# Five re-orderings around waits of TensorE in a two-stack transformer kernel

## What is computed

```
x = x + mamba2_mixer(rms_norm(x, a_norm), ...)   # ends in: groups of y normed, then y @ w_out
x = x + conv_ffn(rms_norm(x, ffn_norm[0]), ...)  # up_a, down
x = x + dilated_mixer(rms_norm(x, b_norm), ...)  # ends in: o @ w_o          (att_o)
x = x + conv_ffn(rms_norm(x, ffn_norm[1]), ...)
for l in range(2):
    h = h + mixer_sublayer(rms_norm(h), ...)
    h = h + memory_cross_attention(rms_norm(h), rms_norm(mem), ...)
    h = h + conv_ffn(rms_norm(h), ...)           # u = h @ w_up; silu(conv(gate)) * val; @ w_down   (up_b, down)
def _rms_norm(x, w, eps): return x * rsqrt(mean(x * x) + eps) * w
```

## Time and profile before

| what | us |
| --- | --- |
| median of 3 runs | 2086.16 |
| lowest and highest | 2086.12 and 2088.02 |
| the profiled execution | 2087.74 |
| its span, first to last instruction | 2085.9 |
| TensorE busy in it | 2067.2 |
| VectorE, ScalarE, GpSimd busy | 1666.1, 1058.4, 256.7 |

### The profile page before, as it was taken

One profiled execution on the slowest core, in us unless ns is written; L12 is line 12 of the kernel. 1 busy time (PEld: TensorE's weight loads), 2 busy tenths in 40 slices (PEclk: granted clock), 3 DMA queues, 4 the chain that ended last, 5 costly groups with the idle time before them and its releaser, 6 DMA issues.

```text
span 2085.9 us, 38628 instructions
## 1 busy us (share of the span) xinstructions
PE 2067.2 (99%) x16378; PEld 2016.3 (97%) x16378; DVE 1666.1 (80%) x2449; ACT 1058.4 (51%) x1282; POOL 256.7 (12%) x176
## 2 busy tenths in 40 slices
PE   9999999999999999999999999999999999999998
PEld 9999999999999999989999999999988999989998
DVE  8987888788769778898986768768698996748765
ACT  6886444457744435355545445434346445445432
POOL 0112055000004510001201001100000301000100
PEclk9999999999999999999999999999999999999999
DMA  7663544563325455443555434445554454534542
GB/s 263 197 205 144 184 182 172 179 216 142 122 102 193 160 188 214 172 181 142 199 186 175 169 142 176 176 165 212 182 182 142 182 185 181 182 131 174 196 144 104
DMA packets 58300, 361.95 MB, mean 174 GB/s; under 512 B 6736, under 2 KB 9360, under 8 KB 21136
## 3 DMA queue, kind: packets, MB, share of 16 engines
q1 hardware_dynamic: 58128, 359.48, 48.4%
HBM read 358.37 MB, written 1.08 MB: 172 GB/s over the span
## 4 chain that ended last, share of the span: by engine, by line
PE 94%; DVE 3%; ACT 1%; issue 1%; POOL 0%; DMA 0%; SPq 0%; DVEq 0%; ACTq 0%
PE acc L639 77%; PE acc L638 7%; PE acc L756 1%; PE acc L755 1%; PE acc L754 1%; DVE w_lo L1192 1%; PE acc L959 1%; ACT w_hi L2059 1%; PE pA L1008 1%; PE pC L802 0%; PE pB L1032 0%; PE pB L1119 0%; PE pD L1119 0%; PE pB L1094 0%; PE pA L1094 0%
## 5 line engine op out<-in xcount | busy, mean ns | idle before, releaser
L639 PE MATMUL acc<-in_hi,w_hi 128*128 128x256 f32 x4656 | 1306.7, 286 | 6.5 <-DVE in_hi L1280 3.8
L639 PE MATMUL acc<-in_hi,w_lo 128*128 128x256 f32 x4656 | 1295.8, 284 | 0.1
L639 PE MATMUL acc<-in_lo,w_hi 128*128 128x256 f32 x4656 | 1233.0, 284 | 0.0
L2059 ACT CAST w_hi<-raw 128x2048 fp32r<-128x2048 f32 (+1 forms) x341 | 615.4, 1805 | 634.8 <-PE acc L639 541.2
L1192 DVE TENSOR_TENSOR w_lo<-raw,w_hi 128x2048 fp32r<-128x2048 f32 (+1 forms) x341 | 739.5, 2169 | 229.3 <-ACT w_hi L2059 228.3
L639 PEld LDWEIGHTS acc<-in_hi,w_hi 128*128 128x128 f32 x4656 | 894.2, 192 | 10.0 <-DVE in_hi L1280 4.0
L639 PEld LDWEIGHTS acc<-in_hi,w_lo 128*128 128x128 f32 x4656 | 894.2, 192 | 0.6 <-DVE w_lo L1524 0.3
L639 PEld LDWEIGHTS acc<-in_lo,w_hi 128*128 128x128 f32 x4656 | 856.7, 192 | 1.2 <-issue 1.0
L2663 POOL TENSOR_TENSOR in_lo<-arena,in_hi 128x256 fp32r<-128x256 f32 (+1 forms) x112 | 139.0, 1241 | 1202.4 <-ACT in_hi L2521 509.9
L1839 DVE SCALAR_TENSOR_TENSOR arena<-arena,cols 128x256 f32<-128x256 f32 x480 | 200.3, 487 | 0.0
L2673 POOL TENSOR_TENSOR arena<-arena 128x256 f32<-128x256 f32 x44 | 84.7, 1925 | 393.0 <-ACT arena L2343 393.0
(11 more groups left out here) (293 smaller groups left out, 1629.3 us busy)
## 6 DMA issues: line engine op xcount, KB each, us to landing
raw<-in_wide SPq DMA_DIRECT2D x285, 1024.0 KB, 4.8
raw<-in_narrow SPq DMA_DIRECT2D x64, 704.0 KB, 4.0
arena<-cs_rows SPq DMA_DIRECT2D x16, 256.0 KB, 4.6
arena<-in_mem SPq DMA_DIRECT2D x3, 1024.0 KB, 4.8
x<-in_x SPq DMA_DIRECT2D x4, 256.0 KB, 6.2
raw<-in_wide SPq DMA_DIRECT2D x2, 512.0 KB, 5.8
tables<-in_tables SPq DMA_DIRECT2D x1, 1024.0 KB, 14.9
arena<-cs_rows SPq DMA_DIRECT2D x16, 64.0 KB, 5.6
```

The lines of the kernel that those rows point to most:

```text
L639: return mm(outs[m], w[:, k, at], moving[:, c, :], start=start, stop=stop)
L2059: copy(w_hi[s][:, 0:n], raw[g % RAW][:, 0:n]).then_inc(hi_ready, 1)
```

## The change

Five edits, all in the order of instructions or in the engine that does them. No matmul is added or taken away.

1. The low parts of the last two of the eight groups go from GpSimd to VectorE, behind its scaling of the groups and ahead of the split of the third `ssm_out` unit. A semaphore `group_low` signals them, and TensorE's late groups 6 and 7 wait on it.
2. `memory_stats` moves from behind unit 6 of the first `down` to behind unit 8, the root from unit 7 to 9, the reciprocal from 7 to 10.
3. In `att_o`, the split that stood between unit 2's early input and its sum of squares goes behind the last unit's early input, just ahead of the split that is there already.
4. In `ffn_b` ScalarE loads the silu table by a one-column activation (`silu_table`) right after the norm, ahead of the next unit's cast.
5. In `ffn_b` VectorE's `norm` leaves out `split(3)` (`leave=True`). It stands now behind the first unit's convolution, with that unit's multiplication (`second`) right behind it, and `split(4)` after both.

```diff
--- before.py
+++ after.py
@@ -363,6 +363,7 @@
         group_sq = sem("group_sq")
+        group_low = sem("group_low")
         rest_in = sem("rest_in")
@@ -455,7 +456,7 @@
             count["all"] += n
-            count[maker] += n
+            count[maker] += n - 2 if name == "groups" else n
@@ -889,7 +890,9 @@
                 early_groups = parts("groups", 0, 4, 2, gin_ready)
-                late_groups = parts("groups", 0, GROUPS_S, 2, gin_ready)[4:]
+                late_groups = parts("groups", 0, GROUPS_S - 2, 2, gin_ready)[4:]
+                late_groups += [(range(2 * g, 2 * g + 2), piece["groups"][0] + g + 1, group_low, g - GROUPS_S + 3)
+                                for g in (GROUPS_S - 2, GROUPS_S - 1)]
                 seg, unit, groups = units("ssm_out")
@@ -898,7 +901,7 @@
                 groups(1, early_groups)
-                E.passed(gin_ready, GROUPS_S)
+                E.passed(gin_ready, GROUPS_S - 2)
                 E.passed(y_ready, GROUPS_S)
@@ -916,7 +919,7 @@
             def memory_stats(u, j):
-                if j == 6:
+                if j == 8:
                     pe.wait_ge(sq_sum, 2)
@@ -1205,6 +1208,7 @@
                     banks = banks_of(seg.base + j)
+                    last_sum = name == "att_o" and u == seg.units - 1
                     fixed = isinstance(u, int)
@@ -1222,15 +1226,20 @@
                             scale_unit(seg, nth, 2)
+                        if early and u == 0:
+                            split(3, seg, 3)
+                            second(u, j, banks)
                         if u < 3:
...
                             split(9, seg, 9)
-                    if ahead and not late:
+                    if last_sum:
+                        split(u + 1, seg, j + 1)
+                    if ahead and not late and not (name == "att_o" and u == seg.units - 2):
                         split(u + 2, seg, j + 2)
-                    if second:
+                    if second and not (late and behind and early and u == 0):
                         second(u, j, banks)
@@ -1259,7 +1268,7 @@
                     tt(sq[:, 0, :], sq[:, 0, :], sq[:, 1, :], ALU.add).then_inc(sq_sum, 1)
-                if j == 7:
+                if j == 10:
                     reciprocal_std(rmem[:])
@@ -1387,7 +1396,7 @@
-            def norm(name, nth, chunk0=0):
+            def norm(name, nth, chunk0=0, leave=False):
@@ -1397,7 +1406,8 @@
                 scale_unit(seg, nth, 1)
-                split(3, seg, 3)
+                if not leave:
+                    split(3, seg, 3)
                 low_parts(xn, chunk0, NORM_PIECES, DC // NORM_PIECES, first=half)
@@ -1615,6 +1625,11 @@
                 group_scaled(1)
+                for g in (GROUPS_S - 2, GROUPS_S - 1):
+                    dve.wait_ge(inh_ready, piece["groups"][0] + g + 1)
+                    at = DC + 2 * g if g < 7 else 0
+                    tt(in_lo[:, at:at + 2, :], xbc[:, 2 * g:2 * g + 2, :], in_hi[:, at:at + 2, :], ALU.subtract
+                       ).then_inc(group_low, 1)
                 E.passed(inh_ready, GROUPS_S)
@@ -1667,7 +1682,7 @@
                 def run():
-                    norm(f"f_norm{l}", 5 + 3 * l)
+                    norm(f"f_norm{l}", 5 + 3 * l, leave=True)
                     hid0 = made["hid"][2 + l]
@@ -2352,7 +2367,7 @@
                     def beside(u, j, banks):
-                        if layer == 0 and j == 7:
+                        if layer == 0 and j == 9:
                             norm_root()
@@ -2361,9 +2376,15 @@
+            def silu_table():
+
+                E.settle()
+                E.mark(fn(act_scratch[:], wcol("eps_rms"), ACT.Silu))
+
             def ffn_b(l):
...
                     norm()
+                    silu_table()
                     base = take.base()
@@ -2700,9 +2721,9 @@
                     ssd_mask(g)
-                for g in range(GROUPS_S):
+                for g in range(GROUPS_S - 2):
                     pool.wait_ge(inh_ready, piece["groups"][0] + g + 1)
-                    d = slice(DC + 2 * g, DC + 2 * g + 2) if g < 7 else slice(0, 2)
+                    d = slice(DC + 2 * g, DC + 2 * g + 2)
                     tt(in_lo[:, d, :], xbc[:, 2 * g:2 * g + 2, :], in_hi[:, d, :], ALU.subtract).then_inc(gin_ready, 1)
...
```

## The result

| | median, us | lowest to highest | runs |
| --- | --- | --- | --- |
| before | 2086.92 | 2086.12 to 2088.02 | 6 |
| changed | 2080.28 | 2079.80 to 2080.63 | 6 |

The ratio is 0.9967, with a 95% interval of 0.9958 to 0.9977. The change takes 6.64 us off the median. The forecast was 2079.0 with a range of 2077.0 to 2082.2, so the time is 1.3 us above the forecast and inside its range. It lies at the very edge of the narrower range, 2077.8 to 2080.3, that the forecast was given for itself.

A forecast was written before the change was run, and what follows sets the result against it. TensorE, busy 2067.2 of 2085.9 us, bounds the kernel, so only its waits and the slow clock behind them count. 3.49 + 0.80 + 1.86 + 1.78 = 7.93 us gave 2079.8 or 2078.2; forecast the middle, 2079.0, range 2077.0 to 2082.2.

The forecast's parts named there:

- Edit 1, 3.49 us: Late groups: 1.90 us of wait and 1.59 us of half clock both go; bounds 0.3 and 3.49.
- the rule of exclusion: Late groups: two-input VectorE and GpSimd operations exclude each other for a whole instruction; VectorE's parts done at 197.1 and 197.75.
- Edit 2, 0.80 us: First `down`: TensorE's wait for the memory sum, matmul at 395.08 instead of 394.28, goes; bounds 0 and 0.80.
- Edit 3, 1.86 us of 5.52: `att_o`: of 3.92 us wait and 1.60 us clock loss, 1.86 us gained; a new wait precedes the statistic.
- Edits 4 and 5, 1.78 us: `up_b`: the fifth unit's wait for the first unit's bank goes, 0.89 us in each layer; bounds 0 and 1.78.
- Edit 5 alone would meet the table load: `up_b`: without the early silu table, moving the split runs into ScalarE's table load; both edits needed for 1.78 us.
- (a): Rival, `att_o`: the clock falls again after the shortened wait and gives back 1.6 us: 2080.6; chance 0.17.
- (b): Rival, late groups: GpSimd's second part is held at the port; 2080.7 with half of 3.49, 2082.2 nearly all; chance 0.13.
- (c): Rival, `up_b`: the gain is given back one unit later, where only 0.5 us are spare: 2080.8; chance 0.05.
- (d): Rival, all stretches: waits only move, VectorE behind by more than one instruction: 2083 to 2085; chance 0.04.
- (e): Rival, `up_b`: slower, fifth unit's split held behind the first convolution, TensorE waits for weights: some 2091; chance 0.02.
- (f): Rival, `att_o`: both waits pass without a slow stretch elsewhere, median stays at its lower level: below 2077.8; chance 0.05.

The follow-up runs named there:

- one group: Changed kernel with only the last group's low part on VectorE, the seventh's on GpSimd as before: 2079.76 us in one execution.
- the two versions with the sums ahead: Changed kernel, `att_o`'s last sums of squares ahead of the second split: 2078.65 us; also third unit's sums behind the last early input: 2078.34 us.
- the first set: Unedited kernel before, run beside the first of three sets of experiments: 2087.01 us, 25 runs.
- the idle products: Kernel before with 8 idle products of `ones` ahead of the last group's wait and 17 ahead of `att_o`'s: 2085.19 us, ratio 0.9990.
- 30 idle products: Kernel before with 14 idle products of `ones` ahead of the last group's wait and 30 ahead of `att_o`'s: 2088.82 us, ratio 1.0007.

## Why the prediction was right, point by point

**What bounds the kernel.** That only TensorE's waits and its slow stretches count held in every run. In the profiles the removed waits moved what follows by their own length, and adding matmuls in waits of before made it 1.81 us faster (0.2 to 4.0).

**Edit 1, 3.49 us.** In the profile it is exact: 3.49 in the changed kernel, and 3.49 alone. VectorE's two parts were done at 197.66, where the rule of exclusion gave 197.75 and the free case 196.9. The half splits came at 198.80 and 199.93, the first at the foreseen 198.9. But the term was mis-sized for a median. Its 1.59 us of half clock was read from one execution and counted as always there, and by the clocks of the 55 runs of before it is there in a third of them at most. Two of the six profiles with this wait lost 2.00 us. Edit 1 alone measured 2.69 us in medians (0.4 to 4.4); 2.00 + 1.49 / 3 would be 2.50. The two parts of the term, wait and clock, should have had chances of their own.

**Edit 2, 0.80 us.** 0.89 between the landmarks on either side of it, and the wait is off the list. It wasn't tried alone.

**Edit 3, 1.86 us of 5.52.** The mechanism and the size are as predicted: 1.86 alone, 2.00 in the changed kernel. Set against the 4.04 us by which the changed kernel leads when it gets there, TensorE was to go on at 604.3 - 4.04 = 600.26 and the statistic to come at 610.55 - 4.04 = 606.51. These are the rows of the changed kernel:

```profile
600.12 0.39 PE L640 MATMUL acc<-in_hi,w_hi 128*128 128x256 f32 x1 [1.44 <-DVE in_hi L1289]
```
```profile
606.37 0.48 PE L770 MATMUL pA<-arena,ones 128*128 128x256 f32 x1 [1.65 <-DVE arena L1353]
```

600.12 and 606.37, both 0.14 us sooner. On VectorE the reason stands in plain sight: the last sum of squares comes behind both splits, together 4.49 us.

```profile
601.03 4.49 DVE L1195 TENSOR_TENSOR w_lo<-raw,w_hi 128x2048 fp32r<-128x2048 f32 x2
605.44 0.88 DVE L1353 TENSOR_TENSOR arena<-arena 128x256 f32<-128x256 f32 x2
```

**Edits 4 and 5, 1.78 us.** 0.91 and 0.90 in the changed kernel. The times of the chain hold too. The bank was to be free 1.4 us ahead of its need (1268.1 for 1269.53); it is free at 1261.94 and used at 1263.53, 1.6 us ahead:

```profile
1259.33 2.28 DVE L1195 TENSOR_TENSOR w_lo<-raw,w_hi 128x2048 fp32r<-128x2048 f32 x1
1261.53 0.41 DVE L1699 TENSOR_TENSOR arena<-arena,acc 128x256 f32<-128x256 f32 x1
```
```profile
1263.53 0.28 PE L640 MATMUL acc<-in_hi,w_hi 128*128 128x256 f32 x1
```

"Edit 4 alone gains nothing" held. "Edit 5 alone would meet the table load" is the one step that was wrong in what it implied. I had put the load where it stood in before, at 1267.85, behind a cast. But edit 5 brings the convolution forward by 2.2 us, and the load goes with it, to 1265.59. With both edits together it is the pair that was priced, so the sum didn't suffer.

**The sum.** 7.93 predicted, 7.84 between the two profiled executions. With the 0.47 us that the changed execution lost ahead of all edits, the edits together brought 8.31. The medians are 6.64 apart. The profile of before lies 0.82 above its median of six (2087.74 and 2086.92), that of the changed kernel 0.38 below its own (2079.90 and 2080.28); together 1.20, which is the difference. That is only the arithmetic; behind the first part stands that this execution had both slow stretches and most runs of before lack one. The prediction had seen that 2087.74 was 1.58 above the median of three, the size of one stretch at half clock, and took the middle for it. The better case was "if the median's runs lacked one, the gain is less by that": it gives 2079.8, and 2080.28 was measured. The middle was a choice without a row behind it, and the range was wide enough for either case. In medians the parts add up: 2.69 + 1.92 + 1.27, and 0.80 for edit 2, are 6.68. With an interval of some 2 us to each side of every one of them, a sum this close to 6.64 is luck.

**The rivals.** (a) A second fall of the clock in `att_o` happened in one execution (one group), and it cost nothing, for the reason given against it: the slow stretch lies in the second wait. The price of 1.6 us was wrong. (b) The port decided nothing; it was VectorE's part that was held, and the first half split was where it had been foreseen. (c) The second unit's bank in `up_b` was free at 1268.35 + 0.41 = 1268.76 and used at 1269.29 without a wait: the 0.5 us to spare are there. (d) and (e) didn't occur. (f) didn't either in this kernel, but the two versions with the sums ahead reach 2078.65 and 2078.34.

## The scatter between executions

Before's 25 runs of the first set spread over 2.4 us (2085.91 to 2088.33), the changed kernel's six and five over 0.8 and 0.9, though fewer runs spread less by themselves. Two causes can be seen in profiles.

One is the slow stretch behind the wait at the groups, 1.5 us, which comes in some executions and not in others. With the idle products in its place, 9 of 11 runs of before lay within 0.7 us (2084.73 to 2085.39). It isn't all: with edit 1 alone, where that wait is gone, ten runs still spread over 2.9 us (2083.85 to 2086.75).

The other is at 80 us, far ahead of all edits. VectorE and GpSimd each have one operation there, and the starts are so close that either can be first. VectorE's operation takes 0.42 us if it comes first. If GpSimd's does, it takes:

```profile
79.80 2.55 DVE L1462 TENSOR_TENSOR arena<-arena 128x256 f32<-128x256 f32 x1
```
```profile
79.67 2.40 POOL L2702 TENSOR_TENSOR arena<-arena,tables 128x1024 f32<-128x1024 f32 x1 [10.76 <-DMA arena<-cs_rows]
```

These are from the kernel with 30 idle products. In before GpSimd started at 79.56, 0.02 us behind VectorE, which kept its 0.42 us, as in ten other profiles of the fourteen. In the changed kernel's first profile GpSimd started at 79.19, VectorE at 79.54, and it took 2.31. GpSimd's start is set by a DMA there, so no edit decides it. At 86 us TensorE is behind before by 0.47 us in the changed kernel's profile, 0.96 with 30 products and 1.12 with edits 4 and 5; 0.15, 0.08 and 0.37 of that are older, so the place costs 0.3 to 0.9 us. Whether moving one of the two would gain this wasn't tried. Nor was what makes the clock fall after one wait of 1.70 us and not after another; that stays open.

## What to carry to other kernels

When a wait on the bounding engine is removed, read where the next input's producer stands on its own engine: here 3.5 of the 5.5 us of the largest wait and its slow stretch stayed, because the next sum stood behind the same two splits. Price a wait and the slow stretch behind it apart, and look at several executions before the second is counted as always there; a few cheap operations for an engine that would idle show what it is worth, once one of them has been timed. A wait that is followed by another wait hides a slow stretch between the two.

## What the runs showed of the hardware

- TensorE's granted clock fell to half (1.2 GHz level, 0.51 to 0.57 over 3.4 to 3.5 us) after every idle of 1.78 to 3.8 us that was looked at, after four of six of 1.7 us, and after none of those of 1.44, 1.45, 1.56, 1.65 and 1.66 us.
- Such a stretch cost 1.5 to 1.6 us at the groups and 1.4 to 1.6 in the six profiles where it stood in front of `att_o`'s statistic and TensorE didn't wait there.
- A VectorE operation of 0.42 us takes 2.3 to 2.55 us when GpSimd's of 2.4 us began first, and 0.42 when it is first by 0.02 us. In the group stage two of 1.29 us took 2.17. The trace agrees with that rule of the Trainium skill in all of them, and a near tie makes it a source of scatter.
- A float32 product with 128 columns of the tile `ones` is two passes of 0.11 us each.
- ScalarE's table load took 1.28 us, and the activation behind it began 0.02 us later.
